# Sums of squares by ones as weights, one product for kk and qk, score pieces of 256 columns, and transposes moved in a hybrid decoder layer

## The reference, cut to what matters

```python
q = l2norm(q.reshape(shp)) * GDN_HEAD_DIM ** -0.5      # x * rsqrt(sum(x*x) + 1e-6)
k = l2norm(k.reshape(shp))
...
a_mat = jnp.where(strict, beta[..., :, None] * jnp.einsum('bhnid,bhnjd->bhnij', k, k) * decay, 0.0)
attn = jnp.einsum('bhnid,bhnjd->bhnij', q, k) * decay
...
p_s = masked_softmax(jnp.einsum('bqghd,bqgmd->bqghm', qg, k_s), mask_s)
...
p_w = masked_softmax(jnp.einsum('bqghd,bkgd->bqghk', qg, kw), mask_w)
o = gt[..., 0:1] * o_c + gt[..., 1:2] * o_s + gt[..., 2:3] * o_w
```

## Time and profile before

| | us |
|---|---|
| median of 3 runs (2278.83 to 2281.86) | 2279.41 |
| the profiled execution, its own time | 2276.04 |
| its span, first to last instruction | 2274.3 |
| PE busy, share of the span | 92% |
| DVE busy, ACT busy | 38%, 26% |

### The profile page before, as it was taken

The page is one execution under the profiler, slowest core; times in us unless marked ns, Lnnn a source line. Parts: engine busy times, 40 slices in busy tenths (PEclk is TensorE's granted clock), DMA queues, the critical chain, the costliest instruction groups (busy, mean ns, idle before and its releaser), DMA issues. The chain is left out here.

```text
span 2274.3 us, 37951 instructions
## 1 busy us (share of the span) xinstructions
PE 2099.0 (92%) x16201; PEld 1417.5 (62%) x16201; DVE 857.9 (38%) x2180; ACT 583.1 (26%) x1481; POOL 131.7 (6%) x144
## 2 busy tenths in 40 slices
PE   8999999999999998599999999689888999999998
PEld 5666667676766666456666666455666666666543
DVE  3545454545454545301556566534321001010112
ACT  2223232323232222100444444233351000000000
POOL 1001010101000000000000000022220000000000
PEclk9999999999999999799999999889998999999999
DMA  4101010101010100402000000198695211110011
GB/s 134 38 11 49 11 49 12 48 11 48 11 48 21 48 20 2 147 19 68 20 11 10 10 10 1 47 332 297 246 355 180 58 32 32 32 45 20 0 65 60
DMA packets 121584, 151.22 MB, mean 66 GB/s; under 512 B 27865, under 2 KB 105089, under 8 KB 112865
## 3 DMA queue, kind: packets, MB, share of 16 engines
q1 hardware_dynamic: 110724, 76.78, 12.1%
q0 software_dynamic: 10704, 72.16, 8.8%
HBM read 136.83 MB, written 16.26 MB: 67 GB/s over the span
## 5 line engine op out<-in xcount | busy, mean ns | idle before, releaser
L822 PE MATMUL g_ps<-hT,W 128*128 128x352 f32 x1440 | 493.3, 471 | 0.0
L822 PEld LDWEIGHTS g_ps<-hT,W 128*128 128x128 f32 x1440 | 250.0, 191 | 96.6 <-issue 4.0
L2533 DVE SCALAR_TENSOR_TENSOR m_sg<-m_sg,m_ps 128x352 f32<-128x352 f32 x48 | 25.0, 521 | 360.7 <-PE m_ps L2473 360.7
L1551 PE MATMUL p_ps<-hT,Wpair 128*128 128x352 f32 x384 | 124.9, 464 | 0.6 <-PEq L1309 0.6
L2485 PE MATMUL m_ps<-m_Wo,m_mixed 128*128 128x512 f32 (+1 forms) x288 | 124.0, 592 | 1.4 <-DVE m_mixed L2536 1.4
L2499 ACT ACTIVATE m_sg<-m_ps 128x352 f32<-128x352 f32 x48 | 22.2, 463 | 386.8 <-PE m_ps L2466 386.8
L2466 PE MATMUL m_ps<-hT,Wgates 128*128 128x352 f32 x384 | 117.6, 465 | 1.5 <-DVEq L2522 1.5
L2466 PE MATMUL m_ps<-hT,m_Wgates 128*128 128x352 f32 x384 | 115.6, 459 | 0.0
L2466 PEld LDWEIGHTS m_ps<-hT,Wgates 128*128 128x128 f32 x384 | 73.9, 193 | 42.9 <-DVEq L2522 1.7
L2466 PEld LDWEIGHTS m_ps<-hT,m_Wgates 128*128 128x128 f32 x384 | 73.0, 190 | 40.6
L1962 PE MATMUL s_ps<-identity,s_G 128*128 128x128 f32 x512 | 75.0, 289 | 24.9 <-ACT s_XT L2177 19.3
(11 more groups left out here) (411 smaller groups left out, 3363.6 us busy)
## 6 DMA issues: line engine op xcount, KB each, us to landing
W<-in_w_in_dram SPq DMA_DIRECT2D x32, 512.0 KB, 5.5
n_x<-in_x_prompt_dram SPq DMA_DIRECT2D x8, 512.0 KB, 7.7
g_S<-in_state_gdn_dram SPq DMA_DIRECT2D x8, 512.0 KB, 4.1
out_dram<-g_S POOLq DMA_DIRECT2D x8, 512.0 KB, 3.8
Wpair<-in_w_in_dram SPq DMA_DIRECT2D x16, 256.0 KB, 3.9
Wgates<-in_w_in_dram SPq DMA_DIRECT2D x8, 512.0 KB, 5.2
m_Wgates<-in_w_in_dram SPq DMA_DIRECT2D x8, 512.0 KB, 5.2
m_Wo<-in_w_out_dram SPq DMA_DIRECT2D x1, 4096.0 KB, 15.2
```

The costliest lines, as they stand in the source:

```text
L822: ins = pe.matmul(ps[:, k.bank, 0:w], W[:, c_, kt, :], hT[:, kt, t0:t0 + w], start=kt == 0, stop=kt == KT - 1)
L1551: ins = pe.matmul(ps[:, fill_bank(n), 0:w], W[:, "qz".index(x), kt, :], hT[:, kt, t0:t0 + w], start=kt == 0, stop=kt == KT - 1)
```

## The change

Sums of squares: the squares are streamed through 32 columns of ones as weights, 256 tokens per matmul, each of the four matmuls of k (and of q) into another group of 32 output partitions; DVE transposes the results in blocks of 32x32 to bring the sums to one per partition. The tile of 32 sample tokens gets a matmul of its own. Products: one matmul per tile streams q and k together against k (256 columns), in five banks of two tiles, `M4` (tile 8) first. Prompt: score matmuls of at most 256 columns (`PIECE`) in place of 512; `turn_co(j)` moves from the middle of step 2j+4 to the end of step 2j+3; only two filler pieces stay between the two groups of transposes, the others go behind; on DVE the copy of the weights and `weights(j)` move ahead of `maxima(m)`.

```diff
-    dve = ["sk", "sq"] + [f"{x}{u}" for x in "AQ" for u in u3] + [f"Y0{n}" for n in g2]
+    dve = ["sk", "sq", "sm"] + [f"M{u}" for u in (4, 0, 1, 2, 3)] + [f"Y0{n}" for n in g2]
...
+            def sums(i):
+                for n, x in enumerate("kq"):
+                    k, bank = dve_bank(f"s{x}", i)
+                    pe.wait_ge(dve_emptied, k.free)
+                    pe.wait_ge(sq_ready, 2 * i + n + 1)
+                    by_corner = SQ[:, at[x], 0:SEQ].rearrange("p (t b j) -> p b t j", b=4, j=Q)
+                    for b, r in enumerate(corners(0)):
+                        ins = pe.matmul(bank[r, 0:PT * Q], c["ones"][:, 0:Q], by_corner[:, b], start=True, stop=True)
+                    ins.then_inc(dve_filled, 1)
...
+                pe.matmul(bank[0:Q, 0:2 * SAMPLE], c["ones"][:, 0:Q], SQ[:, :, SEQ:T], start=True, stop=True
+                          ).then_inc(dve_filled, 1)
...
+                for q, t in enumerate(two_tiles[u]):
                     r = rows_of(t)
-                    ins = pe.matmul(bank[0:r, q * P:q * P + r], Y3[:, at["k"], t * P:t * P + r],
-                                    other[:, t * P:t * P + r], start=True, stop=True)
+                    ins = pe.matmul(bank[0:r, 2 * q * r:2 * (q + 1) * r], Y3[:, at["k"], t * P:t * P + r],
+                                    Y3[:, 0:2, t * P:t * P + r], start=True, stop=True)
...
+                    v.transpose(turned_sums[:, n, 0:PT, :].rearrange("p t j -> p (t j)"), bank[:, 0:PT * Q]
+                                ).then_inc(dve_emptied, 1)
...
+                step(v.tensor_scalar(ss2[0:SAMPLE, :, PT], turned_sums[0:SAMPLE, :, PT, 0], EPS, None, ALU.add))
+                v.tensor_scalar(ss2[:, :, 0:PT], turned_sums[:, :, 0:PT, 0], EPS, None, ALU.add).then_inc(summed, 1)
...
-                    turn_co(j)
                     values_win(j)
...
-                        for n, kt in fill_at[m]:
+                        for n, kt in fill_at[m][:2]:
                             fill(n, kt)
+                for n, kt in fill_at[m][2:]:
+                    fill(n, kt)
+                j = (m - 3) // 2
+                if m % 2 and 0 <= j < J:
+                    turn_co(j)
```

More of the change, by code:

```diff
@@ L531, in stage_gdn @@
     halves = [range(0, 4), range(4, 8)]
+    two_tiles = [range(2 * u, min(2 * u + 2, TT)) for u in range(5)]
     at = {"q": 0, "k": 1, "v": 2, "z": 3}
@@ L886, in fill @@
                         project(head, x, s, kt, kt + 1)
[L888 to L898, removed]
+                sums(i)
+                products(i, 4)
+                products(i, 0)
                 turn(i, "k", 0)
                 turn(i, "k", 1)
+                products(i, 1)
                 fill(z_parts, 3)
                 turn(i, "k", 2)
-                products(i, "Q", 0)
+                products(i, 2)
                 fill(z_parts, 2)
-                products(i, "Q", 1)
-                products(i, "Q", 2)
+                products(i, 3)
                 level_y(i, 0)
@@ L1562, in scores @@
                     q = qT[r % 2][rows, qt * P:(qt + 1) * P]
-                    slc = [(s_slc[:, k0:min(k0 + 512, w)], q, g.slcT[rows, k0:min(k0 + 512, w)])
-                           for k0 in range(0, w, 512)]
+                    slc = [(s_slc[:, k0:min(k0 + PIECE, w)], q, g.slcT[rows, k0:min(k0 + PIECE, w)])
+                           for k0 in range(0, w, PIECE)]
                     if qt == 0 and gr == 0:
@@ L1572, in scores @@
                     q, w0 = qT[r % 2][rows, qt * P:(qt + 1) * P], (qt + 1) * P - w
-                    win = [(s_win[:, k0:min(k0 + 512, w)], q, g.winT[rows, w0 + k0:w0 + min(k0 + 512, w)])
-                           for k0 in range(0, w, 512)]
+                    win = [(s_win[:, k0:min(k0 + PIECE, w)], q, g.winT[rows, w0 + k0:w0 + min(k0 + PIECE, w)])
+                           for k0 in range(0, w, PIECE)]
                     win.append((s_win[:, CMP:CMP + NCB], q, g.kcT[rows, :]))
@@ L1781, in _ @@
                     weights(j)
+                maxima(m)
+                slc = slc_groups(m - 1) if 0 <= m - 1 < U else []
+                if slc:
+                    turn_out(m - 1, 0)
+                j = (m - 4) // 2
+                if m % 2 == 0 and 0 <= j < J:
+                    output(j)
                 if len(slc) > 1:
```

58 lines of the change are left out of this document (27 added, 31 removed).

## The result

The changed kernel took 2272.76 us in the median of 20 runs, against 2280.8 for the kernel before on the same chip: a ratio of 0.9973, 95% interval 0.9963 to 0.9983. The medians lie 8.0 us apart; by the ratio the gain is 6.2 us (3.9 to 8.4), and a second comparison on another chip gave 0.9978 (0.9965 to 0.9991), 5.0 us. I had forecast 15.4 us. The direction and the range held, but the time lies outside the 2258 to 2270 of the likeliest case, and the gain was 0.3 to 0.5 of the one forecast.

The account below looks back on a forecast made before the run. PE, busy for 92% of the span, was taken to bound the kernel. Delta rule 18 - 10.5 = 7.5 us plus prompt stage 8 us made 15.5 us gained, a median of 2264 us; range for 8 of 10, 2251 to 2275.

Parts of the forecast that it names:

- likeliest case: Whole kernel: the sum of the terms holds, 2264 us, in itself from 2258 to 2270; chance 48%.
- POOL starts ... 1.85 us earlier per head: Delta rule, head start: POOL starts 2.8 us behind the sums' start instead of 4.64; 18 us gained with the half-clock heads.
- rival 2: Delta-rule sums: column groups don't run four at a time, only the prompt gain is left, 2271 us; chance 12%.
- Products: Delta-rule q k and k k products: nothing on PE at equal clock, DVE some 0.3 us more, the gain isn't lost.
- 10.5 us in all: Delta rule: PE idles about 3.1 us per head, the clock falls behind it, costing 1.3 us on average per head.
- Rival 1: Delta rule: the clock holds in most heads, 18 + 8 = 26 us gained, 2253 us; chance 20%.
- rival 4: Delta rule: the clock stays down behind the new idle time, slower, 2287 us at 9 us per head; chance 8%.
- 14 - 3 - 3 = 8 us gained: Prompt stage: 14 us of waiting for the weights' copy removed, less 3 for ACT's copy and 3 at `turn_co`.
- Rival 3: Prompt stage gives nothing through new waits or weight loads, the clock takes most of the rest: 2275 us; chance 12%.
- Sum: Whole kernel: 7.5 + 8 = 15.5 us off the profiled 2276.04 gives 2260.5, as a median 2264 us.

Follow-up runs that it names:

- after_again: The changed kernel measured once more, nothing edited: 2273.09 us, 0.9978 of the kernel before.
- delta_only: The kernel before with only the delta-rule part of the change: 2280.79 us, 1.0002 of the kernel before.
- pieces_512: The changed kernel with score pieces of 512 columns again in place of 256: 2262.98 us, 0.9927 of the kernel before.
- the four of the K and V stage: The changed kernel with 128, 256, 384 or 512 instructions added in PE's DMA wait ahead of that stage: 2266.64, 2273.63, 2264.26, 2271.88 us.
- prompt_only: The kernel before with only the prompt part of the change: 2267.61 us, 0.9956 of the kernel before.
- fill_idle: The changed kernel with a product and two projection pieces moved ahead of the third transpose of k: 2247.66 us, 0.9869 of the kernel before.
- pad_heads: The changed kernel with 18 more 32x32 matmuls (72 instructions) in each head's idle time: 2268.10 us, 0.9955 of the kernel before.
- before_shift: The kernel before with 32 more 32x32 matmuls (128 instructions) at the start of the norm stage: 2281.01 us, 1.0016.
- shift_once: The changed kernel with 32 more 32x32 matmuls (128 instructions) in the first head alone: 2262.21 us, 0.9929 of the kernel before.

## Why the prediction was right in its steps and wrong in its sum

With eight profiled executions of the changed delta rule (the changed kernel, `after_again`, `delta_only`, `pieces_512` and the four of the K and V stage) and two of the old one (before, `prompt_only`) each term can be measured, from the starts of PE's rows, summed over the heads:

| stretch | before | changed kernel | mean of eight (range) | forecast | measured |
|---|---|---|---|---|---|
| sums to third k transpose | 91.5, 93.9 | 74.8 | 75.1 (74.8 to 76.6) | -18 | -17.6 |
| from there to level 1 | 51.2, 51.3 | 58.3 | 61.5 (58.3 to 64.8) | +10.5 | +10.3 |
| level 1 to transposes of v | 100.1, 99.4 | 102.4 | 101.6 (100.0 to 102.7) | 0 | +1.8 |
| from there to the next sums (seven) | 552.4, 552.7 | 554.7 | 555.5 (554.6 to 556.9) | 0 | +2.9 |
| whole stage | 863.1, 863.4 | 858.9 | 862.0 (858.5 to 866.0) | -7.5 | -1.3 |

**"POOL starts ... 1.85 us earlier per head", 18 us**: right. Four column groups do run side by side, so rival 2 is out: the eight sums take 0.96 us where I took 0.87. That leaves at most 0.1 us for the drain that the forecast read out of the earlier trace rows; the rows there (1.68 us for 1.5) don't show what the difference is.

**"Products"**: right in size, for a reason I hadn't written down. The first level's second half now waits 0.70 us for DVE's last product, which PE didn't need so early before; PE reaches it 0.23 us sooner, most of it because tile 8's product now stands ahead of the transposes (the last products ahead of the first level take 0.96 us, 1.16 in the earlier trace rows). Where the clock holds, the stretch to level 1 is 6.51 us, 6.40 before: 0.9 us over eight heads.

**"10.5 us in all" for the clock**: right as a sum, from other factors. It fell in 47 of 64 heads, not in all, and cost 1.6 us each time (8.1 us to level 1 in place of 6.51), not 1.3: 9.4 us per execution. How often it falls is not fixed: four heads in one execution of this program, eight in another. Rival 1 (the clock holds) is no outcome of this kernel, and rival 4 (it stays down) neither. The Trainium skill's rule against idle gaps (TensorE: Matmul & The Clock Gate, Why this matters for your kernels) is borne out in three heads of four, and `fill_idle` shows what following it gives.

**"14 - 3 - 3 = 8 us gained"** in the prompt stage: right in sum, 8.3, but not term by term. The new waits are 3.1 us, not 6 (2.4 ahead of `turn_co`, 0.7 more for ACT's copy), which would leave 10 to 11 of the 14. The rest is the clock, at half for 6.8 us where it was 3.4, and 0.9 for a DMA. With half a packet added (128 and 384) neither is there, and the stage takes 380.8 to 382.6 us, 11 to 12.7 less than before. Rival 3 is out.

**What failed is "Sum"**: 7.5 + 8 taken off the profiled execution's time supposes that everything the change doesn't touch keeps its length. It doesn't. In the delta rule the untouched levels and the state loop lost 4.7 us (and the stage's two ends another 1.3), so that the stage gained 1.3 us and not 7.5; `delta_only` says the same, 1.0002. Behind it 8.3 us gained in the prompt stage became 3.8 by the end of the merge (1201.4 before, 1197.2 to 1198.1 in four executions). 1.3 + 3.8 us is the 5 to 6 us measured.

The second loss is the supply of instructions to PE. The delta rule has 576 instructions fewer, two packets and 64, and so the same code behind it stands elsewhere in its packets. By the count at the first matmul of the prompt stage, modulo 256, from there to the end of the merge in us:

| count | old prompt code | new prompt code |
|---|---|---|
| 55 | before 1201.4 | `pad_heads` 1191.2, `prompt_only` 1194.2 |
| 247 | `delta_only` 1208.3 | changed 1198.1 and 1197.5, 256 and 512 added 1197.3 and 1197.2 |
| 183 | `before_shift` 1208.0 | |
| 119 | | `shift_once` 1190.9, 384 added 1191.1, 128 added 1194.5 |

At one and the same place the new prompt code gives 7 to 11 us, the 8 of the forecast. The step from 55 to 247, which the change brings with it, costs 6.9 us with the old code and 3 to 7 with the new. The kernel before stood well, the changed one stands badly: 128 more instructions cost the first 3 us and give the second 6 to 8, and 11 where they come in the first head; 256 or 512 more do nothing that can be told. The page counted before "issue" among PE's waits at 4.6 us, and I took it as a constant of the kernel. I could have seen that it ends behind packets, and that a change in the number of instructions shuffles it; not in which direction.

The first loss, in the delta rule, is not explained by the place. `pad_heads` gives each head its 72 instructions back, so that every head starts at the same count as before (201, 197, 192 and so on; before 201, 196, 191), and yet level 1 to the transposes of v takes 106.3 us there, 100.1 before. With half a packet more the stage takes 861.9 us before and 860.6 in `shift_once`, so the change gains 1.3 us there too.

**What stays open**: why the clock's half stretches in the prompt and sample stages follow the place in the packet as well (the idle pieces alone explain 2 of the 3 to 7 us), and why the idle pieces grew, and not only moved, in the changed delta rule (4.6 and 4.1 us before and in `prompt_only`, 5.6 in `before_shift`; 7.9 to 11.4 in the eight, 7.8 in `shift_once`, 7.1 in `pad_heads`). That is 3 to 7 us, as much as the untouched parts of the stage lost. The traces give a hint: from the first level to the transposes of v PE has 954 instructions in 14.5 to 18.0 us, some 60 per us, while packets land there 3.9 us apart in the median and in no trace closer than 3.3. That brings 66 per us (an estimate, 256 / 3.9). A stage so near to its supply may lose time when the head's start ahead of it, in which packets can get ahead, becomes shorter. No run here tests that.

## What to carry to other kernels

When a change takes work off the busiest engine, ask what PE does with the time. Here the change left 2.8 us of idle time ahead of one transpose, and moving 2 us of ready work per head into it gave 24 us, four times what the change itself had gained. And when PE is fed by bursts of small matmuls, a change that adds or removes instructions can move the time of later stages by some microseconds, for or against it. Before believing a gain or a loss of a few tenths of a percent, pad the program with half a packet of idle instructions (128 here) where an engine waits anyway, and measure again.

## What the runs showed of the hardware

- PE can stand still between independent matmuls with nothing named, for up to 1.7 us in the delta rule and 2.2 in the sample stage. All 204 pieces of over 0.2 us in the delta rule of sixteen traces start at the same count modulo 256 of PE's instructions, and each of those read ends 1.2 to 1.6 us after a 16 KB packet of the instruction queue has landed. A burst of 33 matmuls of 32x32 in float32 is some 130 instructions in 0.77 us, half a packet, and packets came about 4 us apart there, never closer than 3.3 in any trace.
- The time repeats with 256 added instructions: 0, 256 and 512 gave 0.9978, 0.9975 and 0.9980 of the time before, 128 and 384 gave 0.9950 and 0.9943.
- Eight float32 matmuls of 256 columns in four column groups take 0.96 us from start to start, 0.12 each. One after another they would take 0.43 each, the forecast's estimate from a 352-column matmul's 0.595 us.
- The same program had half clock behind the same transpose in four heads of one execution and in eight of another, which alone is 6.5 us of time (58.3 and 64.8 us to level 1).
